# A decoder layer with 32 experts: a third down row tile in the split form, and expert weights in transfers of 1 MB

## The reference

```python
def expert_rows(args):
    xb, e = args
    hid = jax.nn.silu(xb @ w_gate[e]) * (xb @ w_up[e])
    return hid @ w_down[e]

y_rows = lax.map(expert_rows, (x_rows, block_expert)).reshape(n_rows, d)
y = jnp.zeros_like(xf).at[row_token].add(y_rows * row_weight[:, None].astype(y_rows.dtype))
```

## Time and profile before

| what | us |
|---|---|
| median of 3 runs | 1588.99 (1588.62 to 1591.39) |
| the profiled execution | 1591.58 |
| its span, first to last instruction | 1589.8 |
| PE busy | 1537.6 (97%) |
| DVE busy | 1266.0 (80%) |
| ACT busy | 719.1 (45%) |
| POOL busy | 632.2 (40%) |
| moved by DMA | 300.41 MB, mean 189 GB/s |

### The profile page before, as it was taken

One profiled execution on the slowest core, in us unless ns is written; L12 is line 12 of the kernel. 1 busy time (PEld: TensorE's weight loads), 2 busy tenths in 40 slices (PEclk: granted clock), 3 DMA queues, 4 the chain that ended last, 5 costly groups with the idle time before them and its releaser, 6 DMA issues. The chain is left out here.

```text
span 1589.8 us, 22376 instructions
## 1 busy us (share of the span) xinstructions
PE 1537.6 (97%) x7472; PEld 1226.0 (77%) x7472; DVE 1266.0 (80%) x2307; ACT 719.1 (45%) x1232; POOL 632.2 (40%) x749
## 2 busy tenths in 40 slices
PE   6999999999999999999999988999999999999996
PEld 5788888888888888888888776777777777777774
DVE  6678869878778689697787778898888878888883
ACT  5333233232333332332323445666666666666662
POOL 2232231131231322311312224386666666756664
PEclk9999999999999999999999997999999999999998
DMA  4122231221221222212222756999999999999992
GB/s 162 40 84 70 63 87 43 67 84 57 67 84 46 77 64 62 86 44 67 84 57 67 262 211 235 378 379 371 386 378 374 367 373 366 373 376 374 371 355 68
DMA packets 159425, 300.41 MB, mean 189 GB/s; under 512 B 23420, under 2 KB 88620, under 8 KB 159312
## 3 DMA queue, kind: packets, MB, share of 16 engines
q1 hardware_dynamic: 144320, 273.77, 49.0%
q0 software_dynamic: 14992, 25.22, 4.3%
HBM read 299.15 MB, written 25.43 MB: 204 GB/s over the span
## 5 line engine op out<-in xcount | busy, mean ns | idle before, releaser
L2103 DVE TENSOR_TENSOR gu_lo<-w_gu,gu_hi 128x1024 fp32r<-128x1024 f32 x256 | 306.5, 1222 | 49.8 <-ACT gu_hi L1935 38.0
L1361 PE MATMUL proj<-uTh,wl 128*128 128x512 f32 x768 | 303.3, 395 | 6.2 <-POOL wl L573 3.5
L1363 PE MATMUL proj<-uTh,wh 128*128 128x512 f32 x768 | 299.7, 390 | 0.0
L1362 PE MATMUL proj<-uTl,wh 128*128 128x512 f32 x768 | 299.5, 390 | 0.0
L1935 ACT ACTIVATE gu_hi<-w_gu 128x1024 fp32r<-128x1024 f32 x256 | 261.8, 1055 | 61.0 <-PE g_ps L2008 32.7
L573 POOL TENSOR_TENSOR wl<-raw,wh 128x512 fp32r<-128x512 f32 x96 | 134.5, 1418 | 376.5 <-ACT wh L669 376.5
L722 ACT ACTIVATE xbc<-v 128x512 f32<-128x512 f32 x64 | 40.5, 633 | 318.2 <-DVE v L1068 318.2
L1361 PEld LDWEIGHTS proj<-uTh,wl 128*128 128x128 f32 x768 | 144.5, 188 | 42.7 <-POOL wl L573 8.8
L1363 PEld LDWEIGHTS proj<-uTh,wh 128*128 128x128 f32 x768 | 144.3, 188 | 30.6
L1362 PEld LDWEIGHTS proj<-uTl,wh 128*128 128x128 f32 x768 | 144.5, 188 | 29.7
L1068 DVE SCALAR_TENSOR_TENSOR v<-xr,cw,v 128x512 f32<-128x512 f32 x192 | 146.2, 761 | 6.8
(11 more groups left out here) (313 smaller groups left out, 3153.0 us busy)
## 6 DMA issues: line engine op xcount, KB each, us to landing
w_gu<-in_moe_w_gate_dram SPq DMA_DIRECT2D x128, 512.0 KB
w_gu<-in_moe_w_up_dram SPq DMA_DIRECT2D x128, 512.0 KB
w_d<-in_moe_w_down_dram SPq DMA_DIRECT2D x128, 512.0 KB
raw<-in_ssd_w_in_dram SPq DMA_DIRECT2D x96, 256.0 KB, 3.2
E<-acum_dram SPq DMA_DIRECT2D x64, 256.0 KB, 3.3
EE<-eac_dram SPq DMA_DIRECT2D x112, 64.0 KB, 2.8
raw<-in_ssd_w_out_dram SPq DMA_DIRECT2D x28, 256.0 KB, 2.8
hacc<-in_x_dram SPq DMA_DIRECT2D x8, 512.0 KB, 7.4
```

The costliest lines, as they stand in the source:

```text
L1361: nc.tensor.matmul(out, al, bh, start=start, stop=False)
L1362: nc.tensor.matmul(out, ah, bl, start=False, stop=False)
L1363: return nc.tensor.matmul(out, ah, bh, start=False, stop=stop)
L2103: vec.tensor_tensor(wl[:, j % RING, :], weights.gate_up(b, j), wh[:, j % RING, :].bitcast(F32), ALU.subtract).then_inc(w_lo, 1)
```

## The change

1. Down tile 2 goes to the split form as well, so that DS = 3 and only tile 3 is left in full float32. `d_hi` and `d_lo` still have two places (k % 2). Tile 2 takes the place of tile 0, so PE does the tiles in the order 0, 1, 3, 2, and a new function `split_third` makes tile 2's parts after PE has used tile 0. hTh and hTl grow from 256 to 384 columns, hT shrinks to 128.
2. Where `split_third` stands: on ACT behind silu, the rest of the splits and `turn_x`, ahead of `hid_turned`; on the DVE behind `turn_x`, ahead of hTl.
3. Weight loads are paired: 4 for gate and up and 2 for down for each expert, 1 MB each, with 8 KB for each partition. A load waits for both pieces that it overwrites, and a reader of a piece waits for the load that brings it (`loaded_with`).
4. `per_row` lies in the memory of the router's logits, which are no longer needed.

```diff
+    def leads(j):
+
+        return j % 4 < 2 if j < 8 else j % 2 == 0
...
     def load(self, sp, e, b, j):
 
         if j < 8:
             n = j // 2
-            src = self.src[j % 2][bass.ds(e, 1)].rearrange("e (p k) f -> p (e k) f", p=P)[:, 2 * n:2 * n + 2, :]
-            dst = self.gu[b][:, j % 2, 2 * n:2 * n + 2, :]
+            src = self.src[j % 2][bass.ds(e, 1)].rearrange("e (p k) f -> p (e k) f", p=P)[:, 2 * n:2 * n + 4, :]
+            dst = self.gu[b][:, j % 2, 2 * n:2 * n + 4, :]
...
# SP
-                    for j in range(8):
-                        wait(sp, w_lo, p, b, 8, j + 1 - 16)
+                    for j in (0, 1, 4, 5):
+                        wait(sp, w_lo, p, b, 8, j + 3 - 16)
                         weights.load(sp, e, b, j)
...
-                for k in range(KF):
-                    if k < DS:
-                        wait(sp, d_lo, p, b, DS, k + 1 - 2 * DS)
-                    elif k < KF - 1:
-                        wait(sp, d_used, p, b, KF - 1, k + 1 - 2 * (KF - 1))
-                    else:
-                        wait(sp, y_mm, p, b, 2, -2)
+                for k in (0, 2):
+                    wait(sp, d_lo, p, b, DS, (2, 3)[k // 2] - 2 * DS)
+                    if k:
+                        wait(sp, d_used, p, b, 3, 3 - 6)
                     weights.load(sp, e, b % 2, 8 + k)
...
# ACT
+            def split_third(p, b):
+
+                act.wait_ge(weights.loaded_with(b, 10), val(p, 0, 8, 16))
+                wait(act, d_used, p, b, 3, 1)
+                nc.scalar.activation(dh[:, 0, :], weights.d[b][:, 2, :], ACT.Copy).then_inc(d_hi, 1)
...
                     if (b == 0 or not last) and not opening(p, b):
                         turn_x(p, b, 1)
+                    if b == 1:
+                        split_third(p, 0)
+                    elif p[0] is not None or p[1]:
+                        split_third(shifted(p, -1), 1)
                     if b == 1 and last:
                         split_down(p, 1)
                     hid_turned(p, b)
...
# PE
-                for k in range(KF):
+                for k in DOWN:
...
# DVE
             def split_down(p, b):
 
-                for k in range(DS):
+                wait(dve, y_mm, p, b, 2, 0)
+                for k in range(2):
                     wait(dve, d_hi, p, b, DS, k + 1)
...
+            def split_third(p, b):
+
+                wait(dve, d_hi, p, b, DS, 3)
+                wait(dve, d_used, p, b, 3, 1)
+                vec.tensor_tensor(dl[:, 0, :], weights.d[b][:, 2, :], dh[:, 0, :].bitcast(F32), ALU.subtract).then_inc(d_lo, 1)
...
                         if not opening(p, b):
                             turn_x(p, b, 1)
+                    if b == 1:
+                        split_third(p, 0)
+                    elif p[0] is not None or p[1]:
+                        split_third(shifted(p, -1), 1)
```

More of the change, by code:

```diff
@@ L536, in load_first_experts @@
                 for n in range(3 * (c - 2), min(3 * (c - 1), 16)):
-                    weights.load(sp, n // 8, n // 8, n % 8)
+                    if weights.leads(n % 8):
+                        weights.load(sp, n // 8, n // 8, n % 8)
             def store_u2(k):
@@ L1647, in experts @@
     dh, dl = down_parts
-    DS = dh.shape[1]
+    DS = 3
+    DOWN = (0, 1, 3, 2)
     N = 2 * NT
@@ L1693, in experts @@
         few = sb("few", [P, 16])
-        per_row = sb("per_row", [P, 4, N])
+        per_row = rt.lg[:].rearrange("p i e -> p (i e)")[:, 0:4 * N].rearrange("p (v n) -> p v n", v=4)
         hotx = wide[:, 0:N * P // 2].bitcast(BF16).rearrange("p (n q) -> p n q", n=N)
@@ L1784, in _ @@
                 sp.wait_ge(gathered[b], 16)
-                for j in range(8, NPC):
+                for j in range(8, NPC, 2):
                     weights.load(sp, b, b, j)
@@ L1931, in split @@
             def split(p, b, j):
-                act.wait_ge(weights.loaded[b][j], val(p, 0, 8, 16))
+                act.wait_ge(weights.loaded_with(b, j), val(p, 0, 8, 16))
                 wait(act, w_used, p, b, 8, j + 1 - RING)
@@ L1940, in split_down @@
                     act.wait_ge(wtab_mm, 1)
-                for k in range(DS):
-                    act.wait_ge(weights.loaded[b][8 + k], val(p, 0, 8, 16))
-                    wait(act, d_used, p, b, KF - 1, k + 1 - (KF - 1))
-                    nc.scalar.activation(dh[:, k, :], weights.d[b][:, k, :], ACT.Copy).then_inc(d_hi, 1)
+                act.wait_ge(weights.loaded_with(b, 8), val(p, 0, 8, 16))
+                wait(act, y_mm, p, b, 2, 0)
+                nc.scalar.activation(dh[:, 0, :], weights.d[b][:, 0, :], ACT.Copy).then_inc(d_hi, 1)
+                act.wait_ge(weights.loaded_with(b, 9), val(p, 0, 8, 16))
+                wait(act, d_used, p, b, 3, 2 - 3)
+                nc.scalar.activation(dh[:, 1, :], weights.d[b][:, 1, :], ACT.Copy).then_inc(d_hi, 1)
+            def split_third(p, b):
+                act.wait_ge(weights.loaded_with(b, 10), val(p, 0, 8, 16))
+                wait(act, d_used, p, b, 3, 1)
+                nc.scalar.activation(dh[:, 0, :], weights.d[b][:, 2, :], ACT.Copy).then_inc(d_hi, 1)
             def hid_turned(p, b):
@@ L1981, in _ @@
             h_stored(act)
-            pairs(act, body)
+            last = pairs(act, body)
+            split_third(last, 1)
         @block.tensor
@@ L2027, in down @@
                     else:
-                        pe.wait_ge(weights.loaded[b][8 + k], val(p, 0, 8, 16))
+                        pe.wait_ge(weights.loaded_with(b, 8 + k), val(p, 0, 8, 16))
                     for j in range(2):
@@ L2033, in down @@
                         if k < DS:
-                            nc.tensor.matmul(y[j][:], hTl[:, b, k, :], dh[:, k, cols], start=(k == 0), stop=False)
-                            nc.tensor.matmul(y[j][:], hTh[:, b, k, :], dl[:, k, cols], start=False, stop=False)
-                            mm = nc.tensor.matmul(y[j][:], hTh[:, b, k, :], dh[:, k, cols], start=False, stop=False)
+                            nc.tensor.matmul(y[j][:], hTl[:, b, k, :], dh[:, k % 2, cols], start=(k == 0), stop=False)
+                            nc.tensor.matmul(y[j][:], hTh[:, b, k, :], dl[:, k % 2, cols], start=False, stop=False)
+                            mm = nc.tensor.matmul(y[j][:], hTh[:, b, k, :], dh[:, k % 2, cols], start=False, stop=(k == 2))
                         else:
                             mm = nc.tensor.matmul(y[j][:], hT[:, b, k - DS, :], weights.d[b][:, k, cols],
-                                                  start=False, stop=(k == KF - 1))
-                        if k == KF - 1:
+                                                  start=False, stop=False)
+                        if k == 2:
                             mm.then_inc(y_mm, 1)
-                    if k < KF - 1:
+                    if k != 2:
                         mm.then_inc(d_used, 1)
```

13 lines of the change are left out of this document (9 added, 4 removed).

## The result

The changed kernel takes 1691.7 us (median of 4 runs, 1690.34 to 1695.0) against 1589.89 for the kernel before (4 runs, 1588.62 to 1591.39): ratio 1.0642, 95% interval 1.0628 to 1.0656. It is 101.8 us slower. Forecast were 81 us more, 1670, within 1655 to 1695. The profiled execution took 1690.34 with a span of 1688.5, which is 98.7 more than before's span.

A forecast was written before the change was run, and what follows sets the result against it. PE was taken as the bound, with the loads close behind. The stall's 30 x 2.72 = 81.6 us, small terms cancelling, was taken as +81 on the profiled 1591.58, giving 1672.6 and a median of 1670, range 1655 to 1695 us.

The forecast's parts named there:

- What bounds the kernel: In the experts' stage PE sets the pace at 18.50 us an expert, and the DMA loads follow it closely.
- (1) PE's saving: One down row tile on PE goes from fp32 to split form: 0.3 us less an expert if PE were never held.
- rival A: PE stays the bound and the third d_lo is done by G + 16.4: 18.2 us an expert, 1578 us; chance 4%.
- (2) The third split on ACT: One more d_hi in ACT's queue, about 1.05 us, ends at about G + 15.1 and is free, since ACT idles.
- (3) The ring: PE's tile 2 waits for the DVE's third d_lo: 21.22 us an expert against 18.50, 2.72 more, 30 times.
- Rival B, the clock: PE's clock falls in each new pause before tile 2: 30 x 2.6 = 78 us more, about 1748; chance 7%.
- (4) Transfers of 1 MB: Half as many weight loads, same bytes: they stay hidden, with DMA demand falling to about 321 GB/s.
- The 2.0 us of late data: Time 24 experts took beyond 24 x 18.50 us, which the forecast said may vanish with the change.
- (5) The small terms: Routing-table work in the first five experts adds up to 2 us; the end a few tenths; first loads nothing.

The follow-up runs named there:

- the earlier place: Changed kernel with the third split moved ahead, on ACT behind silu and on the DVE behind hid, before the last gu_lo and xTl: 1614.17 us.
- the late tile 2: Changed kernel with 512 KB loads and PE doing tile 2 of one expert behind piece 3 of the next expert's gate and up: 1592.22 us.

## Why the prediction was right, and where it was off

**What bounds the kernel (PE, with the loads close behind)** held, and "close" was the weightier half. The share of 0.98 or 0.99 left no room: with PE 0.3 us faster the DMA engines set the pace at once (1591), and with the fetches disturbed PE was slower by 12 us.

**(1) PE's saving, 0.3 an expert** is real: 18.20 against 18.50 once nothing else holds it. But rival A's 1578 rested on PE alone. Had the third d_lo been in time, the kernel would have come out at about 1591, no change; of that case the forecast had the mechanism, not the price, for the next bound was not asked for.

**(2) The third split on ACT** is free, as said: 1.07 us, done 3.0 before it is taken up; it ends at G + 14.97, forecast G + 15.1.

**(3) The ring** came as it was worked out, link by link: first gu_lo at G + 2.83 (2.82), third d_lo done at G + 19.19 (19.20), PE on at G + 19.25, a hand-over of 0.06 (0.13), tile 2 1.49 (1.50), hid's transposes 0.39, next G at 21.13 (21.22). So 2.63 more an expert, not 2.72, 30 times. That the wait is the cause is shown by the earlier place (1614) and by the late tile 2 (1592), each with the same work. With the clock kept up the kernel takes 1669.85; the forecast said 1670. The steps on the ring come out; the nearness of the two totals is partly luck, since the ring's terms come to 77.4 and not 81.

**Rival B, the clock, was true in part, and is the step that failed.** It was set against the forecast as all or nothing: 2.6 us in each of 30 pauses, 7%, or none, so that the sum has the clock at 0. It came in fourteen of 30, nine of them among the 24, at 1.6 us each there, 21 us in all. It went wrong in two ways. The row used against it, a clock that held through 2.08 us of idle behind dense matmuls, is one pause, and shorter than the new one; one that held can't exclude that some of thirty fall, and at 1008.28 the clock did fall behind a pause of 2.01 us. And a price for part of the pauses, half of them say, belonged in the sum's range as a term of its own. The range held the result only because it was wide for other terms, which is luck.

**(4) Transfers of 1 MB.** "The loads stay hidden" is right of the loads in this kernel: ACT waits for no weight, and SP's longer wait costs nothing. It isn't enough, though: I had looked at the loads' own readers only, and who suffers is another user of the same engines, POOL's scatter and fetch of the output rows. With PE's pause there is slack to cover it, without it 8 to 12 us come up. The 2.0 us of late data did vanish: 24 x 2.63 + 9 x 1.6 - 2.0 = 75.5, measured 75.8.

**(5) The small terms** were near. The first five experts: 5 x 2.72 + 2 = 15.6 forecast, 13.8 without the clock (109.8 less 96.03). The end: one more ring of 2.6 and 1.5 of clock make the 4.2.

By terms for the profiled executions: ring 77.4 (81 forecast, small terms in it), clock 21.3 (0 forecast), 98.7 in all.

## What to carry to other kernels

An engine's idle time can be used only at the place in its list where the idle time lies. The DVE had over 3 us to spare in each expert, at the turn; 1.22 us of work put before that turn, where another engine comes to it at G + 16.4 and the list at G + 18.0, cost 2.6 us of every expert. So walk the closed ring, from one engine's release through the other's list and back, before believing a busy share; and when the bound is relieved, ask how far the next one is, and what a change to a transfer does to the other users of the same DMA engines.

A wait on TensorE of a few us costs more than its length if the clock falls behind it; price it as a share of the pauses, not as yes or no, and fill it to see what it costs.

## What was not expected of the hardware

- TensorE's clock fell behind nine of 24 pauses of nearly the same length (2.62 to 2.69 us, one 2.97) and with the same work around them. The slow matmuls began 0.6 to 1.6 us after the pause had ended, went on at 1.2 GHz for 3.0 to 3.4 us, and cost 1.6.
- Transfers of 1 MB in place of 512 KB, the same bytes from the same queue, delayed the small indirect transfers of another queue (scatter 7.5 us from issue to landing, 6.4 in before; fetch 7.7 in the changed kernel, 6.5 with its loads at 512 KB) and cost 12 us in the kernel before. With rows of 4 KB they cost 9 us; the median hardly moved there (scatter 6.8, fetch 6.6), but single fetches took up to 10.4. With rows of 8 KB the DMA engines' share was lower for nearly the same rate (0.95 at 369 GB/s, 1.00 at 373), which gained nothing.
- Loads that cover 64 partitions at a time kept the DMA engines at a share of 0.99 and moved 235 GB/s; those over all 128 moved 373 at 1.00. The cause wasn't tried.
